# A two-layer hybrid attention trunk on one core: memory turns and dilated row scores in another stage, head sums in two passes, minus |z| on VectorE

## The reference

```python
h = rms_norm(x, ln_g)
u = einsum('bsd,de->bse', h, w_in)          # q, k, v, z of four branches, 4 x 1024 gate logits
o_sb = stick_breaking(q_sb, k_sb, v_sb)     # 4 heads of 64: a = exp(z + cumulated log_sigmoid(-z))
o_fx = forgetting(rms_norm(q), rms_norm(k), v, log_sigmoid(f + b))
o_dl = dilated_mixture(rope(rms_norm(q)), rope(rms_norm(k)), v)   # 12 heads, dilations 1, 4, 16, one softmax over the three
km, vm = split(rms_norm(mem, mem_ln_g) @ w_mem_kv)                # 256 memory tokens
o_mm = cross_attention(rms_norm(q_mm), rms_norm(km), vm)
merged = sum(sigmoid(gate_b) * ((o_b * silu(z_b)) @ w_br_b) for the four branches b)
x = x + merged @ w_out
```

## Time and profile before

| | |
|---|---|
| median of 3 runs | 1352.54 us (1352.37 to 1352.62) |
| the profiled execution | 1349.81 us |
| its span in the trace | 1348.0 us |
| granted TensorE clock, mean | 0.982 |
| PE busy | 1295.9 us, 96% |
| PEld busy | 1022.6 us, 76% |
| POOL busy | 694.3 us, 52% |
| ACT busy | 684.1 us, 51% |
| DVE busy | 559.3 us, 41% |
| HBM read | 107.04 MB |

### The profile page before, as it was taken

The page is one execution under the profiler, slowest core; times in us unless marked ns, Lnnn a source line. Parts: engine busy times, 40 slices in busy tenths (PEclk is TensorE's granted clock), DMA queues, the critical chain, the costliest instruction groups (busy, mean ns, idle before and its releaser), DMA issues. The chain is left out here.

```text
span 1348.0 us, 17624 instructions
## 1 busy us (share of the span) xinstructions
PE 1295.9 (96%) x6138; PEld 1022.6 (76%) x6138; DVE 559.3 (41%) x929; ACT 684.1 (51%) x1257; POOL 694.3 (52%) x571
## 2 busy tenths in 40 slices
PE   7998989998999999999999999999999999999998
PEld 6777868875677788887887787787666778888876
DVE  5896253354341322223349945334542313222221
ACT  6665333586444645454456643248745355544531
POOL 4687322364242476777457863125633325767662
PEclk9999989999999999999999998999999999999999
DMA  7545311122222244444364452112222223444432
GB/s 229 157 105 135 97 39 32 48 63 54 54 59 53 66 107 113 107 113 113 98 166 128 118 131 58 39 40 60 59 55 56 55 55 88 114 104 110 105 115 86
DMA packets 209888, 120.79 MB, mean 90 GB/s; under 512 B 9736, under 2 KB 200328, under 8 KB 209800
## 3 DMA queue, kind: packets, MB, share of 16 engines
q1 hardware_dynamic: 209800, 119.66, 33.8%
HBM read 107.04 MB, written 6.29 MB: 84 GB/s over the span
## 5 line engine op out<-in xcount | busy, mean ns | idle before, releaser
L1699 POOL TENSOR_TENSOR w_lo<-w_raw,w_hi 128x512 fp32r<-128x512 f32 (+1 forms) x400 | 498.1, 1251 | 596.0 <-ACT w_hi L1173 547.3
L765 PE MATMUL dense<-h_hi,w_hi 128*128 128x512 f32 x1168 | 496.4, 425 | 5.3 <-POOL w_lo L1699 2.8
L765 PE MATMUL dense<-h_lo,w_hi 128*128 128x512 f32 x1168 | 461.9, 395 | 0.0
L765 PE MATMUL dense<-h_hi,w_lo 128*128 128x512 f32 x1152 | 454.5, 395 | 0.0
L765 PEld LDWEIGHTS dense<-h_hi,w_hi 128*128 128x128 f32 x1168 | 223.0, 191 | 70.1 <-issue 15.8
L1173 ACT ACTIVATE w_hi<-w_raw 128x512 fp32r<-128x512 f32 (+1 forms) x401 | 231.8, 585 | 67.5 <-PE dense L765 66.3
L765 PEld LDWEIGHTS dense<-h_lo,w_hi 128*128 128x128 f32 x1168 | 223.4, 191 | 48.5 <-issue 9.7
L765 PEld LDWEIGHTS dense<-h_hi,w_lo 128*128 128x128 f32 x1152 | 219.7, 191 | 48.5
L1461 DVE TENSOR_TENSOR sig<-dense,x_rstd_row 128x512 f32<-128x512 f32 x48 | 33.2, 692 | 207.7 <-issue 118.4
L1226 ACT ACTIVATE sig<-sig 128x512 f32<-128x512 f32 x48 | 30.3, 632 | 123.2 <-DVE sig L1461 123.2
L1463 DVE TENSOR_TENSOR raw<-dense,x_rstd_row 128x512 f32<-128x512 f32 x80 | 54.9, 686 | 80.8 <-PE dense L765 62.4
(11 more groups left out here) (292 smaller groups left out, 2021.1 us busy)
## 6 DMA issues: line engine op xcount, KB each, us to landing
w_raw<-in_w_in SPq DMA_DIRECT2D x292, 256.0 KB, 2.9
w_raw<-in_w_out SPq DMA_DIRECT2D x32, 256.0 KB, 2.9
x_scratch<-v_dil SPq DMA_DIRECT2D x16, 256.0 KB, 3.5
w_raw<-in_w_mem_kv SPq DMA_DIRECT2D x16, 256.0 KB, 2.8
v_dil<-x_scratch SPq DMA_DIRECT2D x16, 256.0 KB, 2.7
turned<-normed SPq DMA_DIRECT2D x48, 64.0 KB, 2.4
inv_den<-o_norm SPq DMA_DIRECT2D x48, 64.0 KB, 2.4
silu_z<-in_mem SPq DMA_DIRECT2D x4, 512.0 KB
```

The costliest lines, as they stand in the source:

```text
L765: return nc.tensor.matmul(o, lhsT, rhs, start=start, stop=stop, skip_group_check=True)
L1699: pool.tensor_tensor(w_lo[:, g % SPLIT_SLOTS, c], w_raw[:, g % RAW_SLOTS, c], f(w_hi[:, g % SPLIT_SLOTS, c]), ALU.subtract).then_inc(w_lo_ ...
```

## The change

- **Memory.** mem_square moves to the end of group 1; mem_scale becomes an ACT operation and moves, with the four mem_t, to the first two tiles of group 2.
- **Group 2** is reordered: v0 to v3, mk0, v4, mk1, v5, mv0, z0, mv1, z1. The 16 dilated row steps and max (now maxima(b)) are strewn among the tiles from v3 on. Group 3 begins with the dilated col steps. Five rooms between max and col go.
- **Maxima.** The second order is turned into bank A1 and not into T.
- **Head sums.** All normed tiles are split in hi and lo (ACT copy, DVE subtraction) and summed by two fp32r matmuls; all of them have lag 2. That is 6 tiles of 512 columns and 2 of 256 in each layer.
- **Stick-breaking.** After block j come 3 - j rooms; 6 rooms at the group's end and not 12. Abs on ACT goes; DVE makes min(-z, z) behind its copy of z, and Exp takes it without the factor -1.

```diff
-ROOM_AT_END = 12
+ROOM_AT_END = 6
+    def maxima(b):
+        for p in range(2):
+            for c in range(N_ATT[b][0]):
+                for e in range(2):
+                    yield ("row", b, 2 * p + e, c)
+        yield from [("room",)] * ROOM
+        yield ("max", b)
@@ scores(b)
+                if s < len(order):
+                    yield from [("room",)] * (TT - 1 - order[s][1])
-        for h, c in by_pair(rows):
-            yield ("row", b, h, c)
-        yield from [("room",)] * ROOM
-        yield ("max", b)
-        yield from [("room",)] * ROOM
@@ dense
-                if waiting[2] and waiting[2][-1].rope:
+                if waiting[2] and waiting[2][-1].normed:
                     add("low", waiting[2][-1])
-                while len(waiting[2]) >= lag and not (...):
+                while waiting[2] and len(waiting[2]) >= max(lag, 1 + waiting[2][0].normed) and not (...):
@@ groups 1 to 4
-    dense([new(kind, DIL, i) for kind in "qk" for i in range(6)], [("room",), ("x_sum",)] + [("room",)] * 6
-          + [("mem_square",), ("mem_scale",)] + [("mem_t", c) for c in range(4)] + [("room",)] * 2, lag=2)
-    dense([new(*t) for v, t in enumerate((("mk", MM, 0), ("mk", MM, 1), ("mv", MM, 0), ("mv", MM, 1)))
-           for t in (("v", DIL, v), t)] + [new("v", DIL, i) for i in (4, 5)] + pair_of("z", DIL), lag=2)
+    dense([new(kind, DIL, i) for kind in "qk" for i in range(6)], [("room",), ("x_sum",)] + [("room",)] * 13 + [("mem_square",)], lag=2)
+    dense([new(*t) for t in (("v", DIL, 0), ("v", DIL, 1), ("v", DIL, 2), ("v", DIL, 3), ("mk", MM, 0), ("v", DIL, 4),
+                             ("mk", MM, 1), ("v", DIL, 5), ("mv", MM, 0), ("z", DIL, 0), ("mv", MM, 1), ("z", DIL, 1))],
+          [("mem_scale",), ("room",)] + [("mem_t", c) for c in range(4)] + [("room",)] * 3 + [*maxima(DIL)], lag=2)
-          [*scores(MM), *scores(FOX)])
+          [*maxima(MM), *[("room",)] * ROOM, *scores(MM), *maxima(FOX), *[("room",)] * ROOM, *scores(FOX)])
@@ PE, post2 of a normed tile
-                        if t.rope:
-                            pe.wait_ge(*square_lo_ready.of(t.n))
-                            hi, lo = square_parts(t)
-                            mm(o, rc(HEADSUM), hi, start=True)
-                            last = mm(o, rc(HEADSUM), lo, stop=True)
-                        else:
-                            pe.wait_ge(*squared.of(t.n))
-                            last = mm(o, f(rc(HEADSUM)), square[...], start=True, stop=True)
+                        pe.wait_ge(*square_lo_ready.of(t.n))
+                        hi, lo = square_parts(t)
+                        mm(o, rc(HEADSUM), hi, start=True)
+                        last = mm(o, rc(HEADSUM), lo, stop=True)
@@ PE, max
-                            wait(pe, turn_ring.before(("max", b, order)))
+                            wait(pe, (turn_ring, out_ring[2])[order].before(("max", b, order)))
-                                last = nc.tensor.transpose(T[...], negmax[:, order, i, :], ident)
+                                last = nc.tensor.transpose((T, A1)[order][...], negmax[:, order, i, :], ident)
@@ ACT
+                    elif kind == "mem_scale":
+                        act.wait_ge(*mem_rstd.of("exp"))
+                        for i in range(2):
+                            act.activation(mem_tok[:, i, :], mem_tok[:, i, :], ACT.Copy, scale=mem_ms[:, i:i + 1])
-                        act.activation(t_, sbz[n % 4][:, w], ACT.Abs).then_inc(z_abs.sem, 1)
                         act.wait_ge(*z_abs.of(key))
-                        act.activation(t_, t_, ACT.Exp, scale=-1.0).then_inc(z_exp.sem, 1)
+                        act.activation(t_, t_, ACT.Exp).then_inc(z_exp.sem, 1)
@@ DVE, sb_z
+                        dve.scalar_tensor_tensor(out=sbt[n % 2][:, w], in0=z, scalar=-1.0, in1=z, op0=ALU.mult, op1=ALU.min)
```

More of the change, by code:

```diff
@@ L134, in scores @@
                             yield ("pair", b, order[s - lag][0])
+                if s < len(order):
+                    yield from [("room",)] * (TT - 1 - order[s][1])
             return
-        rows, cols = N_ATT[b]
-        def by_pair(n):
-            return [(2 * p + e, c) for p in range(2) for c in range(n) for e in range(2)]
-        for h, c in by_pair(rows):
-            yield ("row", b, h, c)
-        yield from [("room",)] * ROOM
-        yield ("max", b)
-        yield from [("room",)] * ROOM
-        order = by_pair(cols)
+        cols = N_ATT[b][1]
+        order = [(2 * p + e, c) for p in range(2) for c in range(cols) for e in range(2)]
         later = []
@@ L189, in dense @@
                 waiting[5] = []
-                while len(waiting[2]) >= lag and not (waiting[3] and waiting[3][-1].rope and waiting[2][0].rope):
+                while waiting[2] and len(waiting[2]) >= max(lag, 1 + waiting[2][0].normed) and not (waiting[3] and waiting[3][-1].rope and waiting[2][0].rope):
                     waiting[3].append(waiting[2].pop(0))
@@ L449, in build @@
         squared = signal("squared", normed_tiles)
[L450 to L451 removed]
+        square_hi_ready = signal("square_hi_ready", normed_tiles)
+        square_lo_ready = signal("square_lo_ready", normed_tiles)
         head_summed = signal("head_summed", normed_tiles)
@@ L567, in build @@
             elif s == ("max", DIL):
-                turn_users += [(("max", DIL, 0), max_kept, DIL), (("max", DIL, 1), max_ready, DIL)]
+                turn_users.append((("max", DIL, 0), max_kept, DIL))
+                out_users[2].append((("max", DIL, 1), max_ready, DIL))
             elif s[0] == "max":
@@ L636, in square_parts @@
         def square_parts(t):
-            return [part[:, square_ring.slot(t.n), :] for part in (og_dil_hi, og_dil_lo)]
+            i = square_ring.slot(t.n)
+            if t.rope or t.kind == "mk":
+                return [part[:, i, 0:t.width] for part in (og_dil_hi, og_dil_lo)]
+            return [part[:, 4 + i, :] for part in (dq_hi, dq_lo)]
         def cosine_place(t):
@@ L984, in _ @@
                         for order in range(2 if b == DIL else 1):
-                            wait(pe, turn_ring.before(("max", b, order)))
+                            wait(pe, (turn_ring, out_ring[2])[order].before(("max", b, order)))
                             for i in range(TT):
-                                last = nc.tensor.transpose(T[0:NH, i * P:(i + 1) * P], negmax[:, order, i, :], ident)
+                                last = nc.tensor.transpose((T, A1)[order][0:NH, i * P:(i + 1) * P], negmax[:, order, i, :], ident)
                             last.then_inc(max_turned.sem, 1)
@@ L1234, in _ @@
                                        ACT.Square).then_inc(squared.sem, 1)
[L1235 to L1238, removed]
+                        act.wait_ge(*squared.of(t.n))
+                        act.activation(square_parts(t)[0], square[:, square_ring.slot(t.n), 0:t.width], ACT.Copy)\
+                            .then_inc(square_hi_ready.sem, 1)
                     elif kind == "post2" and s[1].normed:
@@ L1422, in _ @@
                                 .then_inc(out_copied[0], 1)
-                    elif kind == "mem_scale":
-                        dve.wait_ge(*mem_rstd.of("exp"))
-                        for i in range(2):
-                            dve.tensor_scalar(mem_tok[:, i, :], mem_tok[:, i, :], mem_ms[:, i:i + 1], None, ALU.mult)\
-                                .then_inc(mem_scaled.sem, 1)
                     elif kind == "mem_t":
@@ L1515, in _ @@
                         dve.wait_ge(*square_hi_ready.of(t.n))
-                        dve.tensor_tensor(lo, square[:, square_ring.slot(t.n), :], f(hi), ALU.subtract)\
+                        dve.tensor_tensor(lo, square[:, square_ring.slot(t.n), 0:t.width], f(hi), ALU.subtract)\
                             .then_inc(square_lo_ready.sem, 1)
```

14 lines of the change are left out of this document (9 added, 5 removed).

## The result

The kernel with the change took 1345.29 us (median of 5 runs, 1341.93 to 1347.8), the kernel before beside it 1352.54 us (1352.37 to 1352.87). The ratio is 0.9946, with a 95% interval of 0.9932 to 0.996. The forecast was 1325.3 with a range of 1311 to 1342: the sign was right, a gain of 7 us came where 27 were forecast, and the time lies 3.3 us above the range. The profiled span went from 1348.0 to 1343.2 us.

A forecast was written before the change was run, and what follows sets the result against it. PE, busy 1295.9 of 1348.0 us, was taken to bound the kernel through its work, waits and clock. Terms summed to -27.3 us: 1322.5 from the profiled 1349.81, forecast median 1325.3, range 1311 to 1342.

The forecast's parts named there:

- ScalarE copies and later place: Head sums: added ACT copies and DVE subtractions lie beside a 5.5 us tile, covered by the later place; no cost.
- memory's wait and clock in group 1: Memory's first turn: the 5.1 us wait for scaling and two low-clock lengths behind it (3.4) go, -8.5 us.
- scaling late: Memory's first turn in group 2: ACT scales 0 to 1.8 us late, taken as 0.7 a layer.
- w_lo in v3: Behind the memory's four turns sharing one slot, w_lo comes about 1.8 us after PE wants it in v3.
- backlog of VectorE: q and k tiles: scalings leave DVE's fullest stage, so head-sum waits and a low-clock length shrink, -5.0 us (0 to -7.2).
- waits for T and banks, four lengths: Row scores and maxima: waits for T (5.9), banks (1.1 counted) and four low-clock lengths (6.8) go, -13.8 us.
- blocked VectorE: Row steps among group 2's tiles: DVE stops at each four's first step, delaying queued work, +9.8 us (2 to 25).
- stick-breaking: End of stick-breaking: rooms and Abs off ACT remove most of three waits and a low-clock length, -8.5 us (-3 to -9.5).
- The rival in which all eight fours wait: Fours among v, mk and mv tiles: DVE's queue waits behind each, 54 us in place of 9.8, 1369 us; chance 0.07.
- The clock rival: Low-clock lengths move with the small matmuls, not with the waits: +10.2 us, 1335.5 us; chance 0.15.
- That stick-breaking stays as it is: DVE's added step lengthens the chain as much as ACT's lost one shortens it: +8.5 us, 1334; chance 0.10.
- a held-up GpSimd: Added two-SBUF-input DVE operations (48) could each stop a w_lo for 0.7 us: 34 us, 1359; chance 0.03.

The follow-up runs named there:

- experiment 9: all_again's three edits, but one fp32 head sum at the later place in the same banks, without ACT copies and DVE subtractions: 1309.56 us.
- Experiment 3: The changed kernel with the head sums of k1 and q1 of forgetting in bank A1, not T: 1332.24 us.
- experiment 1: The changed kernel with head sums of mk, memory q and forgetting q and k again one fp32 matmul at their old, earlier place: 1336.35 us.
- Edit 6: The changed kernel with the memory's squares and scaling early in group 1 and its four turns six places apart: 1338.19 us.
- Experiment 7: The changed kernel with the four row steps of each burst together at the place of the fourth: 1332.67 us.
- experiments 10: all_again's three edits, but |z| made by ACT again (Abs, Exp with factor -1) and not by DVE: 1305.51 us.
- 11: all_again's three edits, but without rooms behind stick-breaking's blocks and with 12 rooms at the end of group 3; -|z| stays on VectorE: 1308.09 us.
- 5: The changed kernel with the memory's squares and scaling early in group 1 on ScalarE, the turns staying in group 2: 1347.89 us.
- all_again: The changed kernel with row steps in fours, early memory squares and scaling with turns six places apart, and two forgetting head sums in A1, repeated: 1307.16 us.

## Why the forecast was right in sign and wrong in size

Point by point, both layers, forecast and then what the profiles show:

| step of the forecast | forecast | shown |
|---|---|---|
| two passes for one fp32 | -5.7 | -4.5, measured without other waits (experiment 9) |
| wait of q's head sum | -1.6 | -1.6 |
| ScalarE copies and later place | 0 ("covers them") | +11.0 of waits for T, +3.4 of clock |
| memory's wait and clock in group 1 | -8.5 | -8.5 |
| scaling late | +1.4 | +9.5, +3.4 of clock |
| w_lo in v3 | +3.6 | +3.3 |
| backlog of VectorE | -5.0 | -7.2 |
| waits for T and banks, four lengths | -13.8 | -14.3 |
| blocked VectorE | +9.8 | +13.2 (waits 5.0, 4.3 and 0.5, two lengths) |
| first transposed scores | +1.0 | about 0 (waits for VectorE +0.4, for ScalarE -0.5) |
| stick-breaking | -8.5 | -7.3 |

The right column adds up to +0.3; short waits for w_lo of before (3.1) have also gone, and start-up with the first q tile took 1.9 us more, which makes -0.9, and the span shows -4.8. Some 4 us are not placed.

**The step that failed first: "which covers them".** I costed the head sums' later place at nothing because the added operations lie beside a tile of 5.5 us, and counted only when the head sum's *input* is there. The row of the wait shows what was late next: its *output*. ScalarE reads the bank only after the next tile's squares, and the memory maxima want the same bank one place (three matmuls) behind the head sum, v's turn directly behind it. Experiment 3 moves only the bank and gets 13.1 us back; experiment 1 gives up the whole edit and gets 9. Against forecast the step is wrong by 14.4 us.

**The second: "0 to 1.8 us late, I take 0.7 a layer".** The wait was 4.7 and 4.8. I had put ScalarE's own work ahead of the scaling, but not the moved mem_square, which the change puts right there, and not the loop that it opens: the root behind the squares, normed behind the root, the raw copy behind normed, and k5's squares behind the copy. By the estimate above mem_square is 2 us of the wait and VectorE's backlog the larger part; no run moves the squares without the scaling, so this split is read from the trace and not shown by a run. Edit 6 gets 7.1 us back. With the clock behind the wait the term was 11.5 us too small. These two, 25.9 us together, are more than the whole miss (20 in the medians, 22.5 in the spans).

**A size that was off: the blocked VectorE.** Place and price of the first wait were as forecast (2.5), and that of the head sum of mk1 was 1.9 and not 0.65; both layers, not one, had a low length behind v4's start. The rival in which all eight fours wait did not come: negmax releases no dense matmul, and only two places a layer wait for more than 0.3 us. Experiment 7 gives 12.6 us for the whole price, where I had expected 5 to 8, near the 13.2 of the table.

**What held.** Group 1 became 7.9 us shorter in layer 1, against 6.75 forecast and the time of the four turns, which moved. The head sum's two passes are 332.61, 332.84 and the next dense at 333.07, 0.46 us against 0.86 in the earlier trace rows. The Trainium skill (FP8 and Floating Point Precision, "TensorE Precision Notes") gives true fp32 four passes through the array; 0.86 us is close to four times the 0.23 of one fp32r matmul, so the trace agrees. Of the signs, fp32 matmuls were left only for products with v, the start of v4 waited 2.5 us, and stick-breaking kept one wait of about 1 us a layer. The wait at the scaling, one at L988 and ten low lengths in place of six were not what I had named.

**Right by luck.** Waits for w_lo in v3 came at 1.7 a layer against 1.8. I had laid them to four turns close together, but with the turns six places apart the wait is the same 1.7. In both kernels the w_lo that v3 waits for starts 2.8 us after its w_hi is ready (116.6 and 119.4 here), behind a memory lo and a rope product on GpSimd (from 116.1 and 117.7). Stick-breaking came near its number too (7.3 for 8.5), but either of its two edits alone does nearly all of it (experiments 10 and 11).

**The rivals.** The clock rival, that low lengths do not follow waits, does not fit the places that were changed: the lengths at 100, 131 and 360 went whenever the wait ahead of them did. It was only right of the four at the transposed scores. That stick-breaking stays as it is did not come, nor did a held-up GpSimd: a w_lo takes 1268 ns on average after and 1251 before, and the waits for it are no more than forecast. Two things stay open: which of the steps ahead of the w_lo in v3 would have to move, and why a layer has now one and now two or three low lengths at the transposed scores.

## What to carry to other kernels

When an operation is moved, look at both ends of it: when its input is ready, and how long its output holds the bank, with who wants that bank next; here the second was worth more than the whole gain of the edit. In an in-order queue count a moved step among the work ahead of everything that it passes, and put a step that waits for another engine where that engine acts, not where the first part of its data is asked for. Take apart a change of many edits even when it is faster: three small repairs made 1345 into 1307 us, and one edit that was meant to help (-|z| on VectorE) gave nothing once there was room behind the blocks.

## What the runs showed of the hardware

A wait of TensorE of 2.5 to 4.8 us was in six of eight places of the changed kernel behind start-up followed by one length of 3.4 us at 0.50, in which matmuls of 512 columns start 0.43 us apart and not 0.23; it costs another 1.7 us (359.8 to 363.0 above). Not every one: behind the wait of 2.58 us at 336.5 none came, and behind that same wait one came in three other kernels (at 330.7 in experiment 7, 338.6 in 5, 986.8 in 6). The lengths may be why the repairs are worth more together (37.7 us) than one by one (32.8 us).

A two-input operation of VectorE has no one price. min(-z, z) of 512 columns (L1669 in all_again) took 1.04 us on average in stick-breaking. A lo of the squares took 0.75 us at 329.5 but 1.78 us at 90.5 and 1.75 at 98.4, all three in the changed kernel (L1512) and with the same shapes. Why is not shown.
